# Rotation halves by ScalarE and VectorE, and local attention's weights turned by one DMA a slot, in a two-layer mixer trunk

## The reference

```python
def _apply_rope(x, cos, sin):
    x1, x2 = xf[..., :half], xf[..., half:]
    return jnp.concatenate([x1 * c - x2 * s, x2 * c + x1 * s], axis=-1)

def _swa_branch(q, k, v, g, sinks, cos, sin):      # 16 heads of 64, 4 key heads, chunks of 64
    q, k = _apply_rope(...), _apply_rope(...)
    kw, vw = [previous chunk, own chunk] of k and v
    sc = einsum('bclkrd,bcmkd->bckrlm', qc, kw) * HEAD_DIM ** -0.5
    m = maximum(max(sc), sink)
    p = exp(sc - m); p = p / (sum(p) + exp(sink - m))
    o = einsum('bckrlm,bcmkd->bclkrd', p, vw)
    return o * silu(g)
```

## Time and profile before

| | us |
|---|---|
| median of 3 runs | 1915.69 (1913.70 to 1916.15) |
| the profiled execution, its time | 1916.71 |
| its span in the trace | 1914.8 |
| PE busy | 1890.6 |
| DVE busy | 1172.4 |
| ACT busy | 992.4 |
| POOL busy | 393.5 |

### The profile page before, as it was taken

How to read it: one execution, slowest core, us unless ns; L and a number is a source line. 1 busy time by engine, 2 the same in 40 slices (tenths; PEclk the granted TensorE clock), 3 DMA queues, 4 the chain that set the end, 5 groups by cost and what they waited for, 6 DMA issues and landing times.

```text
span 1914.8 us, 27900 instructions
## 1 busy us (share of the span) xinstructions
PE 1890.6 (99%) x11048; PEld 1020.4 (53%) x11048; DVE 1172.4 (61%) x1555; ACT 992.4 (52%) x1912; POOL 393.5 (21%) x266
## 2 busy tenths in 40 slices
PE   7999999999999999999999999999999999999998
PEld 4446765455455664544454477554554555655443
DVE  6677556587436777654367765655873468776432
ACT  5674454465334666543356645544662356765421
POOL 0212021142222332111001130112332222321110
PEclk9999999999999999999999999999999999999999
DMA  6224334443334655434222252354333344554421
GB/s 191 88 88 150 104 106 138 121 122 90 109 105 131 155 128 165 112 132 146 59 67 88 72 166 89 106 150 120 110 105 110 113 137 126 148 138 116 165 84 44
DMA packets 264747, 224.68 MB, mean 117 GB/s; under 512 B 88400, under 2 KB 253226, under 8 KB 264618
## 3 DMA queue, kind: packets, MB, share of 16 engines
q1 hardware_dynamic: 264618, 222.90, 39.3%
HBM read 182.96 MB, written 2.16 MB: 97 GB/s over the span
## 4 chain that ended last, share of the span: by engine, by line
PE 87%; DVE 4%; ACT 3%; issue 2%; POOL 2%; DMA 1%; SPq 1%; DVEq 0%; ACTq 0%; POOLq 0%
PE PS L591 85%; POOL X L1694 1%; DVE Y L1338 1%; DMA X<-X 1%; PE PS L695 1%; DVE X L1338 1%; ACT Y L1077 1%; DVE wsp L1335 1%; SPq L512 1%; DMA stage<-w_in 1%; ACT Y L1078 0%; SPq L564 0%; POOL Y L1694 0%; PE PS L819 0%; ACT wsp L1000 0%
## 5 line engine op out<-in xcount | busy, mean ns | idle before, releaser
L591 PE MATMUL PS<-hT,wsp 128*128 128x512 f16 (+2 forms) x4968 | 1083.2, 377 | 1.0 <-ACT hT L981 1.0
L591 PEld LDWEIGHTS PS<-hT,wsp 128*128 128x128 f16 x4968 | 479.5, 98 | 562.8 <-issue 13.6
L1335 DVE SCALAR_TENSOR_TENSOR wsp<-stage,wsp 128x2048 f16<-128x2048 f32 x148 | 352.9, 2384 | 164.8 <-ACT wsp L1000 162.6
L591 PE MATMUL PS<-ys,wsp 128*128 128x512 f16 x1536 | 339.4, 379 | 0.0
L1000 ACT ACTIVATE wsp<-stage 128x2048 f16<-128x2048 f32 x148 | 281.3, 1901 | 46.6 <-PE PS L591 44.7
L591 PEld LDWEIGHTS PS<-ys,wsp 128*128 128x128 f16 x1536 | 149.4, 98 | 178.4 <-issue 4.1
L591 PE MATMUL PS<-wsp,hT 128*128 128x256 f16 x1728 | 193.2, 273 | 0.0
L591 PEld LDWEIGHTS PS<-wsp,hT 128*128 128x128 f16 x1728 | 168.6, 98 | 22.7 <-issue 2.3
L1003 ACT ACTIVATE X<-PS 128x512 f32<-128x512 f32 (+1 forms) x120 | 68.4, 593 | 140.5 <-PE PS L591 108.2
L1694 POOL TENSOR_TENSOR X<-X,K 128x1024 f32<-128x1024 f32 x26 | 62.7, 2412 | 351.3 <-DMA X<-X 351.3
L1694 POOL TENSOR_TENSOR M<-M,T 128x512 f32<-128x512 f32 x48 | 67.4, 1407 | 292.1 <-DVE T L1335 292.1
(11 more groups left out here) (195 smaller groups left out, 1974.4 us busy)
## 6 DMA issues: line engine op xcount, KB each, us to landing
stage<-w_in SPq DMA_DIRECT2D x120, 1024.0 KB, 5.0
stage<-w_branch SPq DMA_DIRECT2D x32, 1024.0 KB, 5.3
X<-X SPq DMA_DIRECT2D x120, 128.0 KB, 2.4
stage<-w_out SPq DMA_DIRECT2D x8, 1024.0 KB, 5.4
Y<-sums SPq DMA_DIRECT2D x8, 512.0 KB, 6.3
M<-sums SPq DMA_DIRECT2D x8, 512.0 KB, 5.9
Y<-Y SPq DMA_DIRECT2D x24, 128.0 KB, 3.2
xres<-x SPq DMA_DIRECT2D x4, 512.0 KB, 6.7
```

The source lines that it names most:

```text
L591: return pe.matmul(o, a, b, start=start, stop=stop, skip_group_check=True)
L1335: return dve.scalar_tensor_tensor(out=o, in0=a, scalar=c, in1=b, op0=op0, op1=op1)
```

## The change

- **Rotation.** ScalarE makes the hi half of a whole rotated panel in one instruction of 128 partitions into `rhi`; VectorE makes the lo half in one instruction into `rlo` (`rotated_lo`, after `middle`, before the second tile is evacuated). GpSimd's `rotated_lo` is gone. SP now copies both halves to all places: four transfers for a query panel, eight for a key panel.
- **Local attention.** Both units of a slot are handled by one instruction each: maximum (negated by the instruction), sink, sum, reciprocal, multiply. The scores go to banks 4 and 5, and from the second local slot on wait for the exponentials of the slot before (`sw_e`). PE's transposes and ScalarE's copies of them are gone. In their place, in the slot of the scores: ScalarE makes the hi half of `sE` (`local_hi`), VectorE the lo half (`local_lo`), and SP turns both by one DMA_TRANSPOSE of 128x2048 f16 (`turn_local`). The value product is three f16 products per block in place of one in f32; `vc` is kept as hi and lo, the latter made by VectorE.
- **Order on VectorE in a local slot.** `scores_in`, `rotated`, `split_lo`, `before`, `local_gated`, `local_lo`, evacuations.
- `VALUES_AT` goes from 8 to 10.
- The first `gates` wait for `dt_taken`, which the first instruction of the chain gives, not for its end.
- One load of the norm's gains moves to a later turn of SP; the waits that ScalarE had before writing the rotated halves move to SP.

```diff
-VALUES_AT = 8
+VALUES_AT = 10
@@ SP
+                def turn_local(k):
+                    sp.wait_ge(s["sw_hi"], at("sw_hi", k + 1, layer))
+                    sp.wait_ge(s["sw_lo"], at("sw_lo", k + 1, layer))
+                    if k >= 1:
+                        sp.wait_ge(s["sw_o"], at("sw_o", k, layer))
+                    sp.dma_start_transpose(sPT.rearrange("p h e (g n) -> p (h e g) n", n=P), sH.rearrange("p h e n -> p (h e n)"))\
+                        .then_inc(s["sw_turned"], 16)
...
-                            if kind == "kc":
-                                moves = ((kC[other, t], kC[own, t]), (kloC[other, t], kloC[own, t]))
-                            elif kind == "kd":
-                                moves = ((kD[i % 2][other, t], kD[i % 2][own, t]), (kloD[i % 2][other, t], kloD[i % 2][own, t]))
+                            if kind in ("kc", "kd"):
+                                hi, lo = (kC, kloC) if kind == "kc" else (kD[i % 2], kloD[i % 2])
+                                moves = [(to[side, t], of[own]) for to, of in ((hi, rhi), (lo, rlo)) for side in (own, other)]
                             else:
-                                moves = (((qC if kind == "qc" else qD)[i % 2][other, t], by_chunks(kind, rlo[own])),)
+                                to = (qC if kind == "qc" else qD)[i % 2]
+                                moves = [(to[own, t], by_chunks(kind, rhi[own])), (to[other, t], by_chunks(kind, rlo[own]))]
...
                     if DIFF0 <= p - 2 < DIFF0 + 16:
                         turn_differences(p - 2)
+                    if SWA0 <= p - 2 < SWA0 + 8:
+                        turn_local(p - 2 - SWA0)
@@ PE
-                            for g in range(4):
-                                last = pe.transpose(PS[:, 5 + 2 * e, P * g:P * g + P], sE[:, e, g, :], ident)
-                            last.then_inc(s["sw_T"], 1)
...
+                            if n >= 2 and e == 0:
+                                pe.wait_ge(s["sw_e"], at("sw_e", n // 2, layer))
...
-                            pe.wait_ge(s["sw_Ta"], at("sw_Ta", n + 1, layer))
+                            if e == 0:
+                                pe.wait_ge(s["sw_turned"], at("sw_turned", 16 * (n // 2 + 1), layer))
+                                if n >= 2:
+                                    pe.wait_ge(s["sw_y"], at("sw_y", n // 2, layer))
                             for c in range(2):
-                                keys = (vC if c else vE)[:, i, HD * j:HD * j + HD]
-                                for t in range(2):
-                                    o = PS[HD * t:HD * t + HD, 5 + 2 * e, 0:PW].rearrange("p (u n) -> p u n", u=2)[:, :, HD * c:HD * c + HD]
-                                    last = mm(o, keys, sPT[:, e, 2 * c:2 * c + 2, HD * t:HD * t + HD], True, True)
+                                for k, (h, hp) in enumerate(((0, 0), (1, 0), (0, 1))):
+                                    keys = (vC if c else vE)[:, h, i, HD * j:HD * j + HD]
+                                    for t in range(2):
+                                        o = PS[HD * t:HD * t + HD, 6 + e, 0:PW].rearrange("p (u n) -> p u n", u=2)[:, :, HD * c:HD * c + HD]
+                                        exps = sPT[:, hp, e].rearrange("p (g n) -> p g n", n=P)[:, 2 * c:2 * c + 2, HD * t:HD * t + HD]
+                                        last = mm(o, keys, exps, k == 0, k == 2)
...
-                                pe.wait_ge(s["dta_ready"], at("dta_ready", 1, layer))
+                                pe.wait_ge(s["dt_taken"], at("dt_taken", 1, layer))
@@ ACT
-                            copy(sPT[:, e].rearrange("p g n -> p (g n)"), PS[:, 5 + 2 * e, :]).then_inc(s["sw_Ta"], 1)
+                        copy(sH[:, 0], sE.rearrange("p e g n -> p e (g n)")).then_inc(s["sw_hi"], 1)
...
-                    for t in range(2):
-                        copy(dst[HD * t:HD * t + HD, t], by_chunks(kind, rcos[HD * t:HD * t + HD])).then_inc(s["rope_hi"], 1)
+                    copy(rhi, rcos).then_inc(s["rope_hi"], 1)
@@ DVE
+                        link(dve.tensor_reduce(sm, PS[:, 4:6, :].rearrange("p e (g n) -> p e g n", g=4), AX, ALU.max, negate=True))
+                        link(tt(m, m, sink, ALU.min))
+                        tt(d, m, sink, ALU.subtract).then_inc(s["sw_m"], 1)
...
+                        tt(rlo, rcos, rhi, ALU.subtract).then_inc(s["rope_lo"], 1)
...
+                        tt(sH[:, 1], sE.rearrange("p e g n -> p e (g n)"), sH[:, 0], ALU.subtract).then_inc(s["sw_lo"], 1)
...
+                    if SWA0 <= p < SWA0 + 8:
+                        rotated(p)
+                        for n in splits_in(p):
+                            split_lo(n)
                     before(p)
-                    if attention:
+                    if DIFF0 <= p < DIFF0 + 16:
                         rotated(p)
-                    local_gated(p)
-                    if attention:
                         for n in splits_in(p):
                             split_lo(n)
                     differences_lo(p)
+                    local_gated(p)
+                    local_lo(p)
```

More of the change, by code:

```diff
@@ L107 @@
 LOCAL_OUT_AT = 8
+LOCAL_SCORES = 2
 HEADS_AT = 6
@@ L541, in one_layer @@
                         kind, i = PANELS[p - 4][0:2]
[L542 to L543 removed]
+                        sp.wait_ge(s["rope_hi"], at("rope_hi", rope_index(p - 4) + 1, layer))
+                        sp.wait_ge(s["rope_lo"], at("rope_lo", rope_index(p - 4) + 1, layer))
+                        if kind == "qc" and i == 0:
+                            sp.wait_ge(s["ssd_out"], at("ssd_out", 8, layer))
```

230 lines of the change are left out of this document (107 added, 123 removed).

## The result

The changed kernel takes **1924.02 us** (median of five runs, 1921.44 to 1927.87); the kernel before took 1916.14 in the same comparison. The ratio is 1.0048, 95% interval 1.0036 to 1.0060. It is slower by 7.9 us; 1909.5 was forecast, and the time lies outside the range of 1894 to 1920. The profiled execution was the longest of the five (1927.87, span 1926.1, against a span of 1914.8 before).

What follows compares the result with a forecast made beforehand. TensorE's own work and its waits were taken to bound the kernel. Terms -14.0 - 3.2 - 2.4 - 8.4 + 18.4 + 3.4 = -6.2 took the profiled 1916.7 to 1910.5, median 1909.5 us; range 1894 to 1920.

Steps and rivals of the forecast that it cites:

- Transposes: Local slots: TensorE's 128 transposes of 0.109 us each go, -14.0 us.
- Value products: Local slots: 24 f16 products replace f32 ones; -3.2 us if pairs run side by side, +7.2 if not; -3.2 taken.
- Gates of the second layer: Second layer's gates: waiting for the chain's first instruction instead of its end removes 2.4 us of idle time, -2.4.
- Differential attention: Value products at step 10 remove nearly all waits for exponentials and one half-clock stretch: -8.4 us, between 0 and -8.8.
- Rival D: Differential slots: VectorE gets later, so the gain expected there is 0; 1918 us, chance 0.10.
- The new local chain: Local slots 1, 3, 5 of each layer: TensorE waits 2.5, 3.35, 3.35 us for turned weights, +18.4 in two layers.
- The clock: After the six new local waits: two drops to about half clock, 1.7 us each, +3.4; range 0 to 10.
- The rest at nothing: Extra rotated-panel copies on SP, VectorE's lo half of `vc` and the moved gains load cost nothing, having slack.
- B: Local value products: the f16 halves do not run side by side, +10.4 us, 1920; chance 0.10.
- C: Local slots: the turned weights' transfer lands later beside loads; at a landing of 6.0 us, 1928; chance 0.08.
- A: Local slots: transfer in time, no waits, 1887.7 us; 1897 with half the waits; chance 0.16 including shorter landings.

Runs made afterwards that it cites:

- waits_alone: Kernel before with only the differential value products at step 10 instead of 8 and the gates' new wait: 1912.98 us, ratio 0.9986.
- after_sum_behind: Changed kernel with VectorE's sum of the rotated panel moved behind the weights' split and the differences' lo halves in differential slots: 1912.12 us, ratio 0.9981.
- sum_behind: keys_first with VectorE's sum of the rotated panel moved behind the weights' split and the differences' lo halves in differential slots: 1893.67 us, ratio 0.9886.
- keys_first: Changed kernel with VectorE's weights split ahead of the rotation's sum in local slots, and differential key-panel copies ahead of the load on SP: 1898.77 us.
- waits_sum_behind: waits_alone with VectorE's sum of the rotated panel moved behind the weights' split and the differences' lo halves in differential slots: 1926.13 us, ratio 1.0057.
- rotation_waits: Changed kernel without its local part, so the kernel before plus new rotation, value products at step 10 and gates' new wait: 1920.53 us, ratio 1.0028.

## Why the prediction was wrong

Point by point, on the profiled spans (1914.8 and 1926.1).

1. **Transposes, -14.0**: right. No L695 row is left.
2. **Value products, -3.2**: right, and the choice of the end too. A row of 24 takes 0.86 us; from the end of the half product before them (415.57 + 24 x 0.216 = 420.75) to the next product's start at 421.64 it is 0.89, where it was 1.12: -3.7 in 16 slots. The Trainium skill, "TensorEngine Tiling (Array Packing)", Restrictions, says that column tiling switches fast weight loads off. The prediction feared that a load could then last longer than a product, which by its own working would have made the row 1.54 or more; at 0.86 no load shows.
3. **Gates of the second layer, -2.4**: right, 2.5 gone and nothing in its place.
4. **Differential attention, -8.4**: wrong. Waits inside the value products went from 7.2 to 3.8, 2.2 us came at the start of products, and the old half-clock stretch went: -2.9. The step that failed is "VALUES_AT 10 puts six more products (1.3 us) ahead, above the longest wait": it counted what this gives TensorE and not what ends later by it. VectorE's sums of the outputs, the banks they free and the turns of SP all stand behind those products. waits_alone shows it without the rest of the change: 4.9 us off the value products, 6.7 back elsewhere. Rival D had the nearer price (term at 0) with another cause: VectorE has no more work, it has its work in an order with a 4.3 us hole. That the hole is the cause is shown for the new rotation (after_sum_behind, sum_behind). With the rotation of before the same edit lost 13 us, so for waits_alone it is argued.
5. **The new local chain, +18.4**: right in mechanism and place, slots 1, 3 and 5 of each layer, 15.7 us measured in the local slots, 14.5 of it at the value products. The landing was 4.4 where 4.7 was used: six waits of 0.3 less are 1.8 of the difference.
6. **The clock, +3.4**: in the profiled execution four stretches at local waits, +6.8, twice the term. The other executions had about three stretches fewer in all by their mean clock, so for the median the term was nearer. after_sum_behind shows besides that such a stretch and the next wait do not simply add.
7. **"The rest at nothing"**: wrong, and the dearest error. The step that failed is that the pieces of a rotated panel "go out more than a slot before they are read". It does not hold even for query panels: those of slot 0 are issued from 405.71 on, landed at 414.66, and are read at 414.72. The key copies of a head are all issued only at 645.6, 2.3 us before they are due, and the last has landed at 650.5, 4.9 later. Six waits, 10.8 us, and two stretches of 1.7: +14.2. The slack was never read from a row: rows [7] give a query panel's swap for the time of an issue, and no row for the copies. The 4.9 us have their cause in the load just ahead; with the copies ahead of it (keys_first) a copy lands in 2.3 and all six waits are gone.

The sum by these: -14.0 - 3.7 - 2.5 - 2.9 + 15.7 + 6.8 + 14.2 = +13.6, where the spans show +11.3. Of the 2.3 us between them 0.9 lie at the start, where TensorE's 50th instruction comes at 21.47 instead of 22.41; the rest is not accounted for. Against the forecast, term 7 misses by 14.2, term 4 by 5.5, term 6 by 3.4, term 5 by -2.7.

Of the rivals, B (1920) and C (1928) were nearest in time, and neither for its reason: the products do run side by side, and the turned weights landed in 4.4, not in 6.0. But C's mechanism, a transfer that lands late beside a load, is what happened, to the copies of term 7 and not to the turned weights. C's sum also has a slip: at a landing of 5.3 its own price of 0.6 for each 0.1 us gives +3.6 against -6.2, not zero. A, shorter landings, did not happen. The range failed because its slower end was B's price, while "at nothing" stood without a bound.

## What to carry to other kernels

Where an in-order engine stands idle for an operand that another engine delivers, look at what is queued behind it: one line moved (work that is ready ahead of the sum that waits) was worth 19 us in the local slots. In the differential slots the same kind of move was worth 12 in the changed kernel, 5 once the key copies were on time, and it lost 13 where GpSimd still had its long lo halves to do. So try such a move on the kernel as it is to be, with the other orders set. A step placed later in TensorE's stream frees its wait and delays everything that reads its result, so count both. A small copy that is due soon goes ahead of a large load in a queue, unless something shorter still stands behind it, like the sums' write here. And before an item is put down at nothing, find its own row: the time from the last issue to the reader, for the tightest slot, not the one at hand.

## What the runs showed of the hardware

Elementwise instructions of VectorE with two operands in the SBUF last up to 2.2 us longer beside one of GpSimd: 2.79 for two that take 0.62 alone, 2.12 for two that take 0.37, 2.98 for one of 1.22, 3.98 for one of 2.28. GpSimd's product, begun beside such an instruction of VectorE, took 2.99 instead of 2.36 (waits_sum_behind).

A wait alone does not bring the clock down. After TensorE was busy 1.95 of 4 us, and 1.11 of 4, the granted clock fell to 0.52 and 0.56 for 3.4 us. After 2.55 of 4 it did not. Nor did it in rotation_waits, after 1.52 of 4 with a wait of 2.9 us in it (columns as above):

```profile
1594.00:1598.00 4.00, 1.52 (x19) 1.41 (x20) 2.60 (x4) 0.89 (x4) 0.00 (x0) 1.00 0.87 152
```

By the mean clock, the same program had three to seven such stretches from one execution to the next.

Copies of 64 partitions and 128 KB, eight in a row and issued 0.64 us apart, land in a median of 2.3 us ahead of a load of 1 MB (keys_first). Issued behind the load they land in about 5 (changed kernel), and four in a row behind a load in 5.7. Before the change, with two or four in a row, the medians were 2.5 to 3.2.
